# Tensors kept across three stages of a hybrid decoder step: the first head's keys and queries, the samples' value projection, and the output weights

## The reference

```python
z = h @ w_in                                   # columns: retention q,k,v,gate; c_q, c_kv, k_pe; gate; two merge gates
p_ret = (head_rms(retention(q_r, k_r, v_r)) * silu(g_r)) @ w_br_ret
# prompt: per head, causal softmax over q.k with k = [c_kv @ w_uk, k_pe], v = c_kv @ w_uv
# sample: scores against the latent rows themselves, values projected at the end
q_lat = einsum('bthn,chn->bthc', q_nope, w_uk)
p = softmax(concat([q_lat . past_lat + q_pe . past_pe, new], -1) * scale)
o_lat = einsum('bhtk,bkc->bthc', p[..., :P], past_lat) + einsum('bhtk,bkc->bthc', p[..., P:], c_kv)
o = einsum('bthc,chv->bthv', o_lat, w_uv)
p_mla = (o * silu(g_m)) @ w_br_mla
merged = sigmoid(mg_r) * p_ret + sigmoid(mg_m) * p_mla
y = rms_norm(x + merged @ w_out, final_norm_gain)
```

## Time and profile before

| | before |
|---|---|
| median of 3 runs | 2612.98 us (2611.7 to 2613.88) |
| profiled execution, its own time | 2609.06 us |
| its span, first to last instruction | 2607.2 us |
| PE busy | 2422.2 us (93%) |
| DVE busy | 1442.6 us (55%) |
| ACT busy | 1064.6 us (41%) |
| POOL busy | 613.3 us (24%) |

### The profile page before, as it was taken

How to read it: one execution, slowest core, us unless ns; L and a number is a source line. 1 busy time by engine, 2 the same in 40 slices (tenths; PEclk the granted TensorE clock), 3 DMA queues, 4 the chain that set the end, 5 groups by cost and what they waited for, 6 DMA issues and landing times. The chain is left out here.

```text
span 2607.2 us, 42200 instructions
## 1 busy us (share of the span) xinstructions
PE 2422.2 (93%) x15038; PEld 2157.3 (83%) x15038; DVE 1442.6 (55%) x2574; ACT 1064.6 (41%) x2257; POOL 613.3 (24%) x522
## 2 busy tenths in 40 slices
PE   6999999999999999999979998389999995899998
PEld 6999987788877887878868887389999995789887
DVE  3335543355533554345548999278888884333232
ACT  3223432134322343123336665168888883111111
POOL 0023312133201331013315667240000000223222
PEclk9999999999999999999989999689999998899999
DMA  6677776678777876567754442353344304565551
GB/s 174 199 182 214 216 209 177 190 201 226 201 230 194 216 219 195 172 164 203 195 195 141 140 143 65 75 146 84 98 109 110 84 20 131 158 182 156 168 167 51
DMA packets 496001, 417.07 MB, mean 160 GB/s; under 512 B 56113, under 2 KB 447282, under 8 KB 488626
## 3 DMA queue, kind: packets, MB, share of 16 engines
q1 hardware_dynamic: 475874, 393.14, 53.9%
q10 hardware_dynamic: 18768, 17.04, 2.1%
q0 software_dynamic: 1152, 4.19, 0.5%
HBM read 307.52 MB, written 144.49 MB: 173 GB/s over the span
## 5 line engine op out<-in xcount | busy, mean ns | idle before, releaser
L66 PE MATMUL a_bank<-a_h_hi,a_w_hi 128*128 128x512 f32 (+3 forms) x1680 | 608.1, 362 | 21.1 <-DVE a_w_lo L809 15.1
L68 PE MATMUL a_bank<-a_h_hi,a_w_lo 128*128 128x512 f32 (+3 forms) x1680 | 596.0, 355 | 0.0
L67 PE MATMUL a_bank<-a_h_lo,a_w_hi 128*128 128x512 f32 (+3 forms) x1680 | 595.7, 355 | 0.0
L66 PEld LDWEIGHTS a_bank<-a_h_hi,a_w_hi 128*128 128x128 f32 (+1 forms) x1680 | 315.5, 188 | 67.9 <-DVE a_w_lo L809 19.1
L68 PEld LDWEIGHTS a_bank<-a_h_hi,a_w_lo 128*128 128x128 f32 (+1 forms) x1680 | 315.0, 188 | 44.3
L610 ACT ACTIVATE a_w_hi<-a_w_raw 128x1024 fp32r<-128x1024 f32 x168 | 175.0, 1043 | 430.1 <-PE a_bank L68 272.5
L67 PEld LDWEIGHTS a_bank<-a_h_lo,a_w_hi 128*128 128x128 f32 (+1 forms) x1680 | 315.8, 188 | 38.7
L809 DVE TENSOR_TENSOR a_w_lo<-a_w_raw,a_w_hi 128x1024 fp32r<-128x1024 f32 x168 | 204.7, 1219 | 212.6 <-ACT a_w_hi L610 212.5
L1853 ACT ACTIVATE t_prob<-t_bank,t_nm 128x512 f32<-128x512 f32 (+3 forms) x320 | 195.7, 621 | 39.4 <-DVE t_nm L1914 38.7
L1907 DVE TENSOR_REDUCE t_mx<-t_bank 128x1 f32<-128x512 f32 (+3 forms) x320 | 185.8, 603 | 45.6 <-PE t_bank L1965 30.7
L1897 DVE TENSOR_TENSOR t_pt<-t_bank,t_pt 128x512 fp32r<-128x512 f32 (+3 forms) x320 | 188.2, 605 | 27.2 <-ACT t_pt L1839 24.0
(11 more groups left out here) (334 smaller groups left out, 5078.3 us busy)
## 6 DMA issues: line engine op xcount, KB each, us to landing
a_w_raw<-in_w_in SPq DMA_DIRECT2D x164, 512.0 KB, 4.4
between_zT<-a_zo SPq DMA_DIRECT2D x164, 256.0 KB, 3.6
between_LAT<-in_lat_pool SPq DMA_DIRECT2D x256, 128.0 KB, 2.6
p_lat<-between_LAT SPq DMA_DIRECT2D x64, 512.0 KB, 3.1
y_mg<-between_zT SPq DMA_DIRECT2D x112, 128.0 KB, 2.7
t_qt<-between_QT SPq DMA_DIRECT2D x16, 768.0 KB, 11.8
a_x<-in_x_prompt SPq DMA_DIRECT2D x16, 512.0 KB, 5.5
m_zt<-between_zT SPq DMA_DIRECT2D x16, 512.0 KB, 4.7
```

The lines of the kernel that those rows point to most:

```text
L66: pe.matmul(out, lh, rh, start=start, stop=False)
L67: pe.matmul(out, lh, rl, start=False, stop=False)
L68: return pe.matmul(out, ll, rh, start=False, stop=stop)
```

## The change

Tiles that several stages use move into the caller: the constants (`ident`, `hide`, `one_r`), the first head's keys and queries (`head`), and `uv` and `ol`, now already split into high and low. `latent_values` is gone; its parts are spread over the stages around it.

In `attend_paged`: SP, behind its own last load, loads the first head's keys and queries and then `w_uv`, into a part of the `p_lat` buffer. ScalarE makes the high part of the values for odd j, VectorE only for even j and j = 8. The two copies across partitions become reductions. `result` writes a product and its two split parts in place of one product. One more constant is loaded at the start, and GpSimd makes two small copies of constants there.

In `attend`: the head's values get a semaphore of their own (`vin`), and the first scores of head 0 wait for no transfer. A `sample_gate` stands in the streams of TensorE (48 matmuls), VectorE and ScalarE behind step -1. GpSimd loads and splits four more pieces, half of `w_out`, into the head buffers once head 6 is done. In the diff, `values_high` with `a.` is ScalarE's, the first `sample_gate` is VectorE's, and the second, with `three`, TensorE's. SP loads block 0's retention output into `ol`.

In `merge`: TensorE computes the retention branch of k = 0 to 3 of block 0 ahead of everything else, waiting for no transfer. `main(0)` has two transfers fewer. Only two quarters of `w_out` are loaded here, split after k = 1 and k = 7.

```diff
 def attend_paged
+            for x in range(2):
+                sp.dma_start(head[x][0:NOPE].bitcast(F32), T["KT"][0, x]).then_inc(head_in, 16)
+                sp.dma_start(head[x][NOPE:QD].bitcast(F32), T["PE"][x]).then_inc(head_in, 16)
+                sp.dma_start(head[2 + x][0:QD].bitcast(F32), T["QT"][0, x]).then_inc(head_in, 16)
+            grp(sp, "nl", DEC_B - 2, NG)
+            sp.dma_start(uv_raw, T["w_uv"].rearrange("(c p) n -> p c n", p=P)).then_inc(uv_in, 16)
...
+            def values_high(b, u, j):
+                third(a, "tq", b, j, 2)
+                grp(a, "pv", b, j - 3)
+                a.activation(nat[j % 3][0][:], lat[:, u, j * G:(j + 1) * G], ACT.Copy).then_inc(S["nha"], 1)
...
+                if b == DEC_B - 2:
+                    a.wait_ge(uv_in, 16)
+                    a.activation(uv[:, 0], uv_raw, ACT.Copy).then_inc(uv_high, 1)
...
-                    v.tensor_copy(mx[0:NS, u, NU:NG + 1], mx[NS:P, u, 0:NG // 2]).then_inc(S["mxn"], 1)
+                    v.tensor_reduce(mx[0:NS, u, NU:NU + 1], mx[NS:P, u, 0:NG // 2], AX.X, ALU.max).then_inc(S["mxn"], 1)
...
-                v.tensor_copy(total[0:NS, u, NU:NG + 1], total[NS:P, u, 0:NG // 2]).then_inc(S["tc"], 1)
+                v.tensor_reduce(total[0:NS, u, NU:NU + 1], total[NS:P, u, 0:NG // 2], AX.X, ALU.add).then_inc(S["tc"], 1)
...
+                if b == DEC_B - 1:
+                    v.wait_ge(uv_high, 1)
+                    v.tensor_tensor(uv[:, 1], uv_raw, uv[:, 0].bitcast(F32), ALU.subtract).then_inc(uv_low, 1)
...
+                v.tensor_copy(high, own[:]).then_inc(S["fh"], 1)
+                seq(v, "fh", b)
+                v.tensor_tensor(low, own[:], high.bitcast(F32), ALU.subtract).then_inc(S["fin"], 1)
...
-                if at(t - LAG + 1):
+                if opens(t - LAG + 1):
                     values_high(*at(t - LAG + 1))
 def attend
-                for x in range(2):
+                for x in range(2) if h else ():
...
+                if r == 0:
+                    sp.wait_ge(ao_l, 1)
+                    for x, t in enumerate((ao_hi, ao_lo)):
+                        sp.dma_start(T["AOT"][x].rearrange("(k p) t -> p k t", p=P), t).then_inc(ao_st, 16)
+                    for x in range(2):
+                        sp.dma_start(ro0[:, x].bitcast(F32), T["ROT"][x, :, 0:2 * P].rearrange("(k p) t -> p k t", p=P)).then_inc(ro_in, 16)
...
+            def sample_gate():
+                v.wait_ge(gate_in, 16)
+                v.wait_ge(made, 1)
+                for e in range(2):
+                    r = slice(VD * e, VD * e + VD)
+                    v.tensor_tensor(ao[r], bk[r, 7].rearrange("p (a e t) -> p a e t", a=NH // 2, e=2)[:, :, e], gm[r], ALU.mult).then_inc(gated, 1)
+                v.wait_ge(ao_h, 1)
+                v.tensor_tensor(ao_lo.bitcast(F32R), ao, ao_hi, ALU.subtract).then_inc(ao_l, 1)
...
+            def sample_gate():
+                for h in range(NH):
+                    for c in range(2):
+                        f = slice(h // 2 * P, (h // 2 + 1) * P)
+                        i = three(p, bk[:, 7, h * NS:(h + 1) * NS], uv[:, 0, c, f], uv[:, 1, c, f], ol[:, 0, c, h], ol[:, 1, c, h], c == 0, c == 1)
+                i.then_inc(made, 1)
 def merge
+        split_at = {1: 2, DC - 1: 3}
...
-                    if n == 0 and k in (0, 1, 3, 5):
-                        weights((k + 1) // 2)
+                    if n == 0 and k < 2:
+                        weights(2 + k)
                 if n == 0:
-                    sp.wait_ge(wl, len(pieces))
+                    sp.wait_ge(wl, 2)
...
+                ahead = 4 if n == 0 else 0
+                for k in range(ahead):
+                    branch(k, 0)
```

More of the change, by code:

```diff
@@ L1210, in _, with attend_paged @@
                         i.then_inc(lq_made, 1)
-def attend_paged(nc, T, ol):
+def attend_paged(nc, T, ident, hide_r, one_r, head, uv, ol):
     G, NG = 4, N_PAGES // 4
@@ L1400, in exps @@
                 s = side(u, m)
+                if b == 0 and m == 0:
+                    a.wait_ge(ready, 5)
                 if m == 0:
@@ L1695, in decode, with attend @@
-def decode(nc, T):
-    with ExitStack() as ctx:
-        sb, _, _ = kit(nc, ctx)
-        ol = sb("ol", [P, 2, NH, NS])
-        attend_paged(nc, T, ol)
-        latent_values(nc, T, ol)
-def attend(nc, T, early):
+def attend(nc, T, early, ident, hide, one_r, head, vt0, uv, ol):
     G = 4
@@ L1733, in attend @@
         zin = [sem(f"t_zin{u}") for u in range(2)]
-        consts, ready = sem("t_consts"), sem("t_ready")
+        vin, ready = [sem(f"t_vin{u}") for u in range(2)], sem("t_ready")
+        gate_in, made, gated, ao_h, ao_l, ao_st, ro_in = (sem("t_" + x) for x in "gate_in made gated ao_h ao_l ao_st ro_in".split())
         stored = [sem(f"t_stored{x}") for x in range(2)]
@@ L1761, in of_tile, with over @@
             return js[0], js[-1] + 1
-        def over(eng, step):
+        def over(eng, step, sample_gate):
             step(0, -1, True, False, False)
+            sample_gate()
             step(0, 0, True, True, False)
@@ L1885, in step @@
                     exps(1, 1)
+            def sample_gate():
+                a.wait_ge(gated, 2)
+                a.activation(ao_hi.bitcast(F32R), ao, ACT.Copy).then_inc(ao_h, 1)
             a.wait_ge(ready, 1)
-            over(a, step)
+            over(a, step, sample_gate)
         @block.vector
@@ L2013, in step, with merge @@
                     p.transpose(bk[:, 0, 0:P], den[:], ident[:]).then_inc(flipped, 1)
-            over(p, step)
-def merge(nc, T, wr, wm):
+            over(p, step, sample_gate)
+def merge(nc, T, wr, wm, wo_hi, ro0):
     W = 2 * P
@@ L2053, in merge @@
         block = ctx.enter_context(nc.Block())
-        pieces = [(wo, "w_out", c) for c in range(0, DC, 2)]
+        split_at = {1: 2, DC - 1: 3}
         def at(eng, name, n, k=0):
@@ L2284, in pair @@
             return sb(name + "_hi", shape, F32R), sb(name + "_lo", shape, F32R)
[L2286 to L2288 removed]
+        ident, hide, one_r = sb("k_ident", [P, P]), sb("k_hide", [P, P], F32R), sb("k_one", [P, P], F32R)
+        head = [sb("k_" + x, [P, SEQ], F32R) for x in "kt_hi kt_lo qt_hi qt_lo".split()]
+        uv, ol = sb("k_uv", [P, 2, 2, NH * VD], F32R), sb("k_ol", [P, 2, 2, NH, NS], F32R)
+        attend_paged(nc, T, ident, hide, one_r, head, uv, ol)
+        vt0 = sb("k_vt", [P, SEQ], F32R)
+        wr, wm = pair("y_wr", [P, 4, D_MODEL]), pair("y_wm", [P, 4, D_MODEL])
+        out = [[head[2 * i + x][:].rearrange("p (a n) -> p a n", a=2) for i in range(2)] for x in range(2)]
+        early = [([t[:, c:c + 1] for t in w], src, c) for w, src in ((wr, "w_ret"), (wm, "w_mla")) for c in range(4)]
+        early += [([out[x][c // 2][:, c % 2:c % 2 + 1] for x in range(2)], "w_out", c) for c in range(4)]
+        attend(nc, T, early, ident, hide, one_r, head, vt0, uv, ol)
+        uv_flat, ol_flat = uv[:].rearrange("p x c n -> p (x c n)"), ol[:].rearrange("p x c h t -> p (x c h t)")
+        merge(nc, T, wr, wm, [[head[0], head[2], vt0], [head[1], head[3], uv_flat, ol_flat]],
+              ol_flat.rearrange("p (x k t) -> p x k t", x=2, k=4))
 OUTS = (("y_p", (SEQ, D_MODEL), (1, SEQ, D_MODEL)), ("y_s", (NS, D_MODEL), (DEC_B, DEC_T, D_MODEL)),
```

211 lines of the change are left out of this document (99 added, 112 removed).

## The result

The changed kernel takes 2555.45 us (median of 4 runs, 2554.08 to 2557.5), against 2612.34 us in 4 runs of the kernel before: a ratio of 0.9785, 95% interval 0.9772 to 0.9798. The forecast was 2545, range 2527 to 2564: the direction and most of the terms hold, and 11 us of the gain are missing (56.9 us of the 68 forecast). The profiled execution took 2554.55 us, its span 2552.8.

The account below looks back on a forecast made before the run. TensorE, busy 93% of the span, bounds the kernel; gains lie where it waits. Terms -17 + 0.7 - 38 - 14 = -68 take 2609.06 to 2541; medians lie 3.9 higher: 2545 us, range 2527 to 2564.

Parts of the forecast that it names:

- Paged loop: In `attend_paged`: TensorE's waits behind VectorE's two copies mostly go, -17 us, bounds 0 and -23.
- each copy gives back about 1.45 to 1.65 us of VectorE: In `attend_paged`: a 64-partition reduction takes 0.153 us where the copies had medians of 1.80 and 1.60.
- The rule weighed in the prediction: VectorE's copies, casts and operations with two SBUF inputs wait for GpSimd; reductions and ScalarE never; at its fullest 2562 us.
- the 6 us set against it: In `attend_paged`: 4 us for `result`'s new cast and subtract, which can wait for GpSimd, and 2 for residual waits.
- The first rival: In `attend_paged`: the stall only moves, to `result`, and the paged loop gains nothing: 2562 us, chance 0.16.
- the slower case: ScalarE's 32 copies in the paged loop might each wait 2.38 us for GpSimd: 2638 us, chance 0.03.
- Last steps: End of `attend_paged`: some 4 us of GpSimd waits go, ScalarE's wait for `w_uv` costs about as much: 0, bounds -4, +4.
- Stage end: From VectorE's old end in `attend_paged` to the prompt's first scores: 3.9 us in place of 48.5, -44.6.
- Sample gate: In `attend`: its 48 matmuls come back on TensorE's path, 10.3 us at clock 0.50, 5.6 at 1.00; 8 taken.
- A new wait in `attend`: Rival: head 0's values and the samples' gate land late, VectorE, ScalarE and TensorE wait: +6, 2551 us, chance 0.08.
- `merge`, -14 forecast: Start of `merge`: gating starts sooner, two splits replace four, SP goes on at about 2220, not 2234; bounds -8, -17.
- 2 MB, 11 us: Start of `merge`: without the retention output 2 MB load in 11 us, not 3 MB in 16.5; gating starts 5 us sooner.

Follow-up runs that it names:

- e5_uv_copy_later: The changed kernel with ScalarE's copy of `w_uv` moved from in front of sample 6's result to the end of the step behind it: 2553.32 us, ratio 0.978.
- e4_plain_scale: The changed kernel, but block 0 of `merge` reads plain rows of the gate instead of the repeated inverse denominators: 2552.35 us in one run.

## Why the prediction came out 11 us short

- **Paged loop, -17 forecast, -12.1 measured: the step that failed is "each copy gives back about 1.45 to 1.65 us of VectorE".** The stall ends when GpSimd's subtract ends (1511.38 to 1513.77, the addition 1511.91 to 1513.80), so it stays if the next operation behind the copy meets it too. In `whole` that is the addition of the mask, with two SBUF operands, right behind the copy. GpSimd at that place, timeline of the changed kernel:

```profile
1511.38 2.39 POOL L1384 TENSOR_TENSOR p_nat<-p_lat,p_nat 128x1024 fp32r<-128x1024 f32 x1 [0.95 <-PE p_bank L1601]
```

  The rule weighed in the prediction (the Trainium skill, "SBUF — State Buffer", "Who interferes with whom") names such operations; it was applied to `result` alone, where it did TensorE no harm. The traces agree with it: 1.89 us with two SBUF operands, 0.16 with one of them in PSUM. Behind the first copy TensorE got back 0.35 us a sample and not 2.0 (4.62 to 4.28, 4.27 to 4.26), behind the second about the 1.5 forecast (3.87 to 3.47, 5.52 to 4.34). With that addition out of the way the loop from the first to the last small turn is 19.0 us shorter than before (241.46 to 222.44). That this lies near the forecast is in part luck: the gross gain was put at 23, and the 6 us set against it don't show (the step behind a result takes 3.85 us, and took 3.80).
- **The first rival, right in mechanism, wrong in place.** The stall did move, but to the next operation of `whole`, not to `result`: its cast took 1.22 us, and the step with it fell from 5.52 to 4.34.
- **ScalarE's copies**: 1.05 to 1.08 us for 32, never longer; the slower case has no support.
- **Last steps, 0 forecast**: the last small turn to the last result's matmul went from 37.5 to 36.2 us. The wait for `w_uv` was there, 3.9 us, in the changed kernel; e5_uv_copy_later didn't get it back.

```profile
1620.50 0.93 PEld L1660 LDWEIGHTS p_bank<-p_fold,p_oc 128*128 128x128 f32 x4 [3.88 <-ACT p_oc L1462]
```

- **Stage end, -44.6 forecast, -45.5 measured**, 1644.40 to 1646.25 being one boundary. **Sample gate**, 8 forecast, 7.1 by this window of the changed kernel. Its clock of 0.74 is a mean: the granted clock is 1.00 from 1652.48 to 1655.77 and 0.50 from 1655.80 to 1659.60, with TensorE busy throughout. The first scores ahead of it, behind the 4 us of standing still, ran at 0.50.

```profile
1652.48:1659.60 7.12, 7.12 (x50) 7.12 (x49) 1.00 (x3) 2.79 (x8) 0.00 (x0) 0.74 1.02 221
```

- **A new wait in `attend`** did not come: none of TensorE's waits there is for a transfer, and the stretch grew by 6.4 us against 6.9 forecast.
- **`merge`, -14 forecast, -6.7 measured: two steps failed.** "2 MB, 11 us": the last input landed after 15.6 us and not 11, since the load of the inverse denominators sets it and not the bytes; with plain rows it is 11.3, in one run. That is 4.3 of the miss. And nothing was charged for where tiles lie: 6 ns for each of 768 matmuls, 4.6 us, of which 3.0 show, net, behind the load of `x`. The splits did as forecast: 15.8 us from the end of the first to the end of the last, 23.9 before, by these rows of the changed kernel. TensorE was busy at the start of the stage, from 2126.30, but stood still again, 15.6 us by the longest wait, for the gating.

```profile
2158.49 2.29 DVE L2243 TENSOR_TENSOR k_uv<-y_x,k_vt 128x2048 fp32r<-128x2048 f32 x1 [3.10 <-ACT k_vt L2202]
...
2174.30 2.29 DVE L2243 TENSOR_TENSOR k_ol<-y_x,y_wo 128x2048 fp32r<-128x2048 f32 x1 [4.12 <-ACT y_wo L2202]
```

## What to carry to other kernels

When a short instruction is slow because it waits, ask which instruction behind it waits for the same thing, and price the removal of the whole chain. Price a load whose last piece is late by its own landing time and by the DMA share while all wait, not by bytes. And when tiles move in SBUF, compare the distance of successive matmul starts: it can change by nearly 3% (227 to 233 ns) with no wait to show it.

## What was not expected of the hardware

- Where tiles begin in SBUF sets the pace of matmuls in `merge`. Those of 512 fp32r columns started every 227 ns in the runs where the quarters of `w_out`, high and low, and the rows `m_hi` and `m_lo` all begin at addresses equal modulo 512, and every 233 where seven of the eight quarter tiles differ from the rows by 32 or 64 bytes; there the matmuls with the eighth, which does not differ, were 1 to 3 ns quicker than the others and not 6. Those of 256 columns started every 117 ns where weights and rows differ by 32, and every 120 where they begin equal. Only these orders were tried, and neither the rule nor its reason is settled.
- While the repeated rows of the inverse denominators are outstanding, the share of 0.24 is what four of the 16 DMA engines would give, busy all the time (0.24 x 16 = 3.8). The Trainium skill, "DMA: Bandwidth & Descriptors", "Rules for kernel authors", says that an outermost dimension below 16 confines a transfer to at most that many engines; here 64 repeats stand outermost and 4 heads inside. The plain rows of e4_plain_scale were loaded in that same order, 64 outermost and 4 inside, and the share there was 1.12: the order alone does not do it. How the repetition would, no run here shows.
